# Attention groups put between the gate projections, in the second block of a two-block model

## What is computed

```
h = rms_norm_2(x, attn_norm_g[i])
proj = h @ w_in[i]
q, k, v, f_logit, cb, cc, cu, ga, gb = jnp.split(proj, offs, axis=-1)

q = rms_norm_2(q.reshape(b, s, N_ATT_HEADS, HEAD_DIM), q_norm_g[i])
k = rms_norm_2(k.reshape(b, s, N_ATT_HEADS, HEAD_DIM), k_norm_g[i])
log_f = jax.nn.log_sigmoid(f_logit.astype(jnp.float32) + b_f[i].astype(jnp.float32))
y_att = forgetting_attention(q, k, v, log_f)      # 8 heads of 64, causal, blocks of 128 queries

y_conv = cb * causal_short_conv(cc * cu, conv_w[i])

merged = (jax.nn.sigmoid(ga) * (y_att @ w_out_att[i])
          + jax.nn.sigmoid(gb) * (y_conv @ w_out_conv[i]))
x = x + merged @ w_o[i]
```

## Time and profile before

| | us |
|---|---|
| median of 3 runs | 1838.84 |
| lowest, highest | 1838.61, 1843.57 |
| the profiled execution | 1839.28 |
| its span in the profile | 1837.6 |

### The profile page before, as it was taken

One profiled execution on the slowest core, in us unless ns is written; L12 is line 12 of the kernel. 1 busy time (PEld: TensorE's weight loads), 2 busy tenths in 40 slices (PEclk: granted clock), 3 DMA queues, 4 the chain that ended last, 5 costly groups with the idle time before them and its releaser, 6 DMA issues.

```text
span 1837.6 us, 24106 instructions
## 1 busy us (share of the span) xinstructions
PE 1696.0 (92%) x9603; PEld 1372.4 (75%) x9603; DVE 1286.6 (70%) x1152; ACT 1000.6 (54%) x850; POOL 23.9 (1%) x37
## 2 busy tenths in 40 slices
PE   6989999997999999999999999999699978799977
PEld 6969998886676767767676766767499947688856
DVE  5974445895887878788787878878547424577773
ACT  4644433553776767667676767667334322266642
POOL 3000000000000000000000000000000000000000
PEclk9999999997999999999999999999899957799998
DMA  9535555422889979898997989898645502288850
GB/s 288 183 118 175 185 194 187 141 90 103 296 303 335 370 261 367 312 330 306 333 350 285 373 300 336 304 334 328 195 146 176 184 1 92 81 272 276 275 185 23
DMA packets 240762, 431.54 MB, mean 235 GB/s; under 512 B 11540, under 2 KB 121648, under 8 KB 240688
## 3 DMA queue, kind: packets, MB, share of 16 engines
q1 hardware_dynamic: 239200, 426.17, 66.0%
q10 hardware_dynamic: 1488, 4.34, 0.7%
HBM read 429.44 MB, written 1.05 MB: 234 GB/s over the span
## 4 chain that ended last, share of the span: by engine, by line
PE 74%; issue 14%; DVE 7%; ACT 3%; DMA 1%; POOL 0%; DVEq 0%; SPq 0%; POOLq 0%; ACTq 0%
PE PS L991 22%; PE PS L993 21%; PE PS L992 21%; DVE w_low L1433 2%; PE PS L1071 2%; PE PS L1205 2%; ACT w_high L799 2%; PE PS L1191 1%; DVE hT_low L1433 1%; PE PS L1370 1%; PE PS L1369 1%; PE PS L1237 1%; PE PS L1385 1%; DMA ring<-in_w_in_dram 1%; DVE yT_low L1433 1%
## 5 line engine op out<-in xcount | busy, mean ns | idle before, releaser
L1433 DVE TENSOR_TENSOR w_low<-ring,w_high 128x2048 fp32r<-128x2048 f32 x402 | 917.2, 2289 | 323.8 <-ACT w_high L663 169.4
L799 ACT ACTIVATE w_high<-ring 128x2048 fp32r<-128x2048 f32 x306 | 585.5, 1917 | 281.4 <-PE PS L993 281.2
L991 PE MATMUL PS<-w_high,hT_high 128*96 128x512 f32 (+3 forms) x1184 | 421.6, 356 | 13.1 <-DVE w_low L1433 8.0
L993 PE MATMUL PS<-w_high,hT_low 128*96 128x512 f32 (+3 forms) x1184 | 413.8, 349 | 0.0
L992 PE MATMUL PS<-w_low,hT_high 128*96 128x512 f32 (+3 forms) x1184 | 412.3, 348 | 0.0
L663 ACT ACTIVATE w_high<-ring 128x2048 fp32r<-128x2048 f32 x96 | 182.9, 1911 | 153.3 <-PE PS L993 149.5
L991 PE MATMUL PS<-w_high,yT_high 128*96 128x512 f32 (+1 forms) x568 | 228.9, 403 | 23.0 <-DVE yT_low L1433 23.0
L991 PE MATMUL PS<-hT_high,w_high 128*128 128x256 f32 x832 | 239.4, 288 | 8.2 <-DVE hT_low L1433 6.4
L991 PEld LDWEIGHTS PS<-w_high,hT_high 128*96 128x96 f32 (+1 forms) x1184 | 196.9, 166 | 64.9 <-DVE w_low L1433 7.7
L992 PE MATMUL PS<-hT_low,w_high 128*128 128x256 f32 x832 | 237.1, 285 | 0.0
L993 PE MATMUL PS<-hT_high,w_low 128*128 128x256 f32 x832 | 237.1, 285 | 0.0
(11 more groups left out here) (287 smaller groups left out, 1328.2 us busy)
## 6 DMA issues: line engine op xcount, KB each, us to landing
ring<-in_moe_wg_dram SPq DMA_DIRECT2D x88, 1024.0 KB, 6.1
ring<-in_moe_wu_dram SPq DMA_DIRECT2D x88, 1024.0 KB, 6.9
ring<-in_moe_wd_dram SPq DMA_DIRECT2D x80, 1024.0 KB, 5.7
ring<-in_w_in_dram SPq DMA_DIRECT2D x36, 1024.0 KB, 5.7
ring<-in_w_gate_dram SPq DMA_DIRECT2D x16, 1024.0 KB, 6.8
ring<-in_w_up_dram SPq DMA_DIRECT2D x16, 1024.0 KB, 7.7
ring<-in_w_down_dram SPq DMA_DIRECT2D x16, 1024.0 KB, 5.2
ring<-in_ffn_wg_dram SPq DMA_DIRECT2D x11, 1024.0 KB, 5.2
```

The lines of the kernel that those rows point to most:

```text
L799: act.activation(w_high[:, (s.base + k) % SPLITS, :], slot(w), ACT.Copy).then_inc(s.high_taken, 1)
L991: mm(o, left_high, right_high, start=first, stop=False, skip_group_check=shared)
L993: return mm(o, left_low, right_high, start=False, stop=last_one, skip_group_check=shared)
L1433: return tt(out_, whole, part.bitcast(F32), ALU.subtract)
```

## The change

TensorE now computes the first logits behind the `cu` tiles, and the rest of the attention in between the eight gate tiles: logits 0, gate 0, logits 1, gates 1 and 2, transposed weights 0, gate 3, weighted values 0, gate 4, transposed y 0 and weights 1, gate 5, weighted values 1, gate 6, transposed y 1, gate 7. The gates use banks 4 and 5 in turn, with one sigmoid of 512 columns per tile; block 0 of the attention uses banks 6 and 7, block 1 banks 0 to 3. ScalarE's and VectorE's lists are put in the matching order, with one `high` or `low` between two steps. `w_out_conv2` and `w_out_att` stand behind each other after the last gate. A new semaphore, `out_att_half`, tells when the first four of eight column chunks of `w_out_att` are complete; VectorE merges the first half on it and the second after the last chunk. `w_o` sums into banks 4 to 7 (before 0 to 3), its first two tiles wait for the first half of the merge alone, and there are 8 idle transposes in place of 16. What each operation computes stays as it was.

```diff
+            def gate(k):
+
+                name = (("ga0", "ga1", "gb0", "gb1")[k // 2], k % 2)
+                used(act, name)
+                act.activation(sgu[:, k // 2, (k % 2) * HALF:(k % 2 + 1) * HALF], bank(4 + k % 2),
+                               ACT.Sigmoid).then_inc(gates_act, 1)
+
...
+            gate(0)
+            high(B + 15)
+            weights_of(0)
+            gate(1)
+            high(B + 16)
+            act.wait_ge(yconv, 1)
+            act.activation(yT_high[:, 4:8, :].rearrange("p c s -> p (c s)"), wk[2], ACT.Copy).then_inc(yconv_high, 1)
+            gate(2)
+            high(B + 17)
+            turned_weights(0)
+            gate(3)
+            high(B + 18)
+            weights_of(1)
+            gate(4)
+            high(B + 19)
+            y_high(0)
+            turned_weights(1)
+            gate(5)
+            high(B + 20)
+            gate(6)
+            high(B + 21)
+            y_high(1)
+            gate(7)
+            high(B + 22)
+            high(B + 23)
...
-            for name, b, freed, value in (("cc", 0, qk_hat, 1), ("cu", 2, qk_hat, 2), ("ga0", 4, cbu_copied, 1),
-                                          ("ga1", 6, qk_std, 2), ("gb0", 0, cc_used, 1), ("gb1", 2, cbu_copied, 2)):
-                pe.wait_ge(freed, value)
+            for name, b, value in (("cc", 0, 1), ("cu", 2, 2)):
+                pe.wait_ge(qk_hat, value)
                 for hf in range(2):
                     project_T((name, hf), b + hf)
+
+            def logits(t):
+
+                n, each, b0 = P * (t + 1), 4 // (t + 1), 0 if t else 6
+                for hd in range(HEADS):
+                    o = PS[:, b0 + hd // each, (hd % each) * n:(hd % each + 1) * n]
+                    mm(o, qz[:, hd, t * P:(t + 1) * P], uT[:, hd // 2, 0:n], start=True, stop=False)
+                    last = mm(o, head_row[0:HEADS, hd, :], negc[:, 0:n], start=False, stop=True)
+                last.then_inc(att_logits, 1)
...
+            def turn_weights(t):
+
+                L, nk = (L1 if t else L0), t + 1
+                pe.wait_ge(att_exp, HEADS * (t + 1))
...
+            def weighted_values(t):
+
+                nk = t + 1
+                pe.wait_ge(att_pT_s, (1, 3)[t])
+                pe.wait_ge(att_pT_v, (1, 3)[t])
...
+            def turn_y(t):
+
+                pe.wait_ge(att_y, t + 1)
+                for c in range(4):
+                    last = nc.tensor.transpose(PS[:, 1 if t else 7, c * P:(c + 1) * P],
+                                               wk[3][:, t * HALF + c * P:t * HALF + (c + 1) * P], ident[:])
...
+            def gate(k):
+
+                if k >= 2:
+                    pe.wait_ge(gates_act, k - 1)
+                project_T((("ga0", "ga1", "gb0", "gb1")[k // 2], k % 2), 4 + k % 2)
+
+            pe.wait_ge(qk_std, 2)
+            logits(0)
+            pe.wait_ge(cbu_copied, 1)
+            gate(0)
+            pe.wait_ge(cbu_copied, 2)
+            pe.wait_ge(cc_used, 1)
+            logits(1)
+            gate(1)
+            gate(2)
+            turn_weights(0)
+            gate(3)
+            weighted_values(0)
+            gate(4)
+            turn_y(0)
+            turn_weights(1)
+            gate(5)
+            weighted_values(1)
+            gate(6)
+            turn_y(1)
+            gate(7)
...
+                        if name == "out_att" and m == 1 and c == 3:
+                            last.then_inc(att_half, 1)
                     last.then_inc(split_used, 1)
 
             pe.wait_ge(yconv_low, 1)
-            pe.wait_ge(gates_act, 2)
+            pe.wait_ge(gates_act, 8)
+            pe.wait_ge(att_yT, 1)
             out_chunks("out_conv2", 4, 4)
...
             pe.wait_ge(att_yT, 2)
             out_chunks("out_att", 0, 0)
             pe.wait_ge(mT_sum, 1)
-            spare(4, 16)
-            pe.wait_ge(merged, 2)
+            pe.wait_ge(conv_gated, 2)
+            spare(4, 8)
             for m in range(4):
-                rows_of_model(("o", m), h_rows, 0, m == 0, m == 3)
+                pe.wait_ge(merged, 1 + m // 2)
+                rows_of_model(("o", m), h_rows, 4, m == 0, m == 3)
...
 
             v.wait_ge(cbu_copied, 2)
             cu = wk[1].rearrange("p (c s) -> p c s", c=CH)
             tt(cpad[:, :, PAD:], chunks(0), cu, ALU.mult).then_inc(cc_used, 1)
             v.wait_ge(cc_used, 1)
-            low(B + 15)
+            low(B + 14)
...
+            def row_maxima(t):
+
+                L, n, each, b0 = (L1 if t else L0), P * (t + 1), 4 // (t + 1), 0 if t else 6
+                v.wait_ge(att_logits, t + 1)
...
+            row_maxima(0)
...
+            low(B + 15)
+            row_maxima(1)
             low(B + 16)
-            low(B + 17)
-            low(B + 18)
             v.wait_ge(yconv_high, 1)
             rest_of(yT_low[:, 4:8, :].rearrange("p c s -> p (c s)"), wk[2],
                     yT_high[:, 4:8, :].rearrange("p c s -> p (c s)")).then_inc(yconv_low, 1)
-            for T in range(19, 24):
-                low(B + T)
+            low(B + 17)
+            turned_weights(0)
+            low(B + 18)
+            scaled_y(0)
+            low(B + 19)
+            y_low(0)
+            turned_weights(1)
+            low(B + 20)
+            scaled_y(1)
+            low(B + 21)
+            y_low(1)
+            low(B + 22)
+            low(B + 23)
...
-                        yT_high[:, 0:4, t * P:(t + 1) * P]).then_inc(att_yT, 1)
-
             low(B + 24)
             low(B + 25)
-            used(v, ("out_att", 1))
-            v.wait_ge(conv_gated, 2)
-            for k in range(2):
+
+            def merge(k):
+
                 own.link(tt(sgu[:, k, :], sgu[:, k, :], bank(2 * k, 2), ALU.mult))
                 tt(sgu[:, k, :], sgu[:, k, :], sgu[:, 2 + k, :], ALU.add).then_inc(mT_sum, 1)
-            for k in range(2):
+
+            def merged_low(k):
+
                 v.wait_ge(mT_high, k + 1)
                 rest_of(hT_low[:, 4 * k:4 * k + 4, :].rearrange("p c s -> p (c s)"), sgu[:, k, :],
                         hT_high[:, 4 * k:4 * k + 4, :].rearrange("p c s -> p (c s)")).then_inc(merged, 1)
+
+            v.wait_ge(conv_gated, 2)
+            v.wait_ge(att_half, 1)
+            merge(0)
+            used(v, ("out_att", 1))
+            merge(1)
+            merged_low(0)
+            merged_low(1)
             for T in range(26, 30):
                 low(B + T)
-            add_rows(0, 3, ("o", 3))
+            add_rows(4, 3, ("o", 3))
...
```

More of the change, by code:

```diff
@@ L276, in build @@
         rows_half, conv_gated, yconv_low = sem("rows_half"), sem("conv_gated"), sem("yconv_low")
+        att_half = sem("out_att_half")
         rest_landed = [[sem(f"rest{k}_landed{s}") for s in range(SLOTS)] for k in (1, 2)]
@@ L908, in _, with weights_of @@
             high(B + 14)
[L909 to L919, removed]
+            def gate(k):
[3 more added lines that the diff above has]
+                               ACT.Sigmoid).then_inc(gates_act, 1)
+            def weights_of(t):
                 L = L1 if t else L0
@@ new lines, in turn_weights @@
+            def turn_weights(t):
+                L, nk = (L1 if t else L0), t + 1
+                pe.wait_ge(att_exp, HEADS * (t + 1))
+                for b in range(2 * nk):
+                    for c in range(4):
+                        hd, kt = (4 * b + c) // nk, (4 * b + c) % nk
+                        last = nc.tensor.transpose(PS[:, (0 if t else 6) + b, c * P:(c + 1) * P],
+                                                   L[:, hd, kt * P:(kt + 1) * P], ident[:])
+                    last.then_inc(att_turned, 1)
@@ new lines, in weighted_values @@
+            def weighted_values(t):
+                nk = t + 1
+                pe.wait_ge(att_pT_s, (1, 3)[t])
+                pe.wait_ge(att_pT_v, (1, 3)[t])
+                for hd in range(HEADS):
+                    for kt in range(nk):
+                        last = mm(PS[:, 0 if t else 6, hd * 64:(hd + 1) * 64], PT[:, hd * nk + kt, :],
+                                  vn[:, kt, hd * 64:(hd + 1) * 64], start=(kt == 0), stop=(kt == nk - 1))
+                last.then_inc(att_out, 1)
@@ new lines, in turn_y @@
+            def turn_y(t):
+                pe.wait_ge(att_y, t + 1)
+                for c in range(4):
+                    last = nc.tensor.transpose(PS[:, 1 if t else 7, c * P:(c + 1) * P],
+                                               wk[3][:, t * HALF + c * P:t * HALF + (c + 1) * P], ident[:])
+                last.then_inc(att_yturned, 1)
+            def gate(k):
+                if k >= 2:
+                    pe.wait_ge(gates_act, k - 1)
+                project_T((("ga0", "ga1", "gb0", "gb1")[k // 2], k % 2), 4 + k % 2)
@@ L1857, in _ @@
                 op1=ALU.mult).then_inc(qk_hat, 1)
-            for T in range(10, 15):
+            for T in range(10, 14):
                 low(B + T)
@@ L1890, in _ @@
             for k in range(2):
```

(10 more changed lines are left out.)

76 lines of the change are left out of this document (28 added, 48 removed).

## The result

| | before | changed |
|---|---|---|
| median, us | 1838.72 (4 runs) | 1814.76 (4 runs) |
| lowest, highest | 1838.37, 1843.57 | 1812.80, 1818.79 |
| the profiled execution | 1839.28 | 1815.69 |
| its span | 1837.6 | 1813.9 |
| mean granted clock | 0.959 | 0.966 |

The ratio is 0.9866, with a 95% interval of 0.9842 to 0.9890: 24.7 us faster by the ratio. The forecast was 1813, with 1801 to 1826 as its range.

The account below looks back on a forecast made before the run. TensorE's work was taken as the bound, leaving its idle and lower-clock time to win. 12.4 + 11.7 - 3.6 + 1.8 + 2.7 + 0.9 = 25.9 us off 1839.3 gave 1813 us, range 1801 to 1826.

Parts of the forecast that it names:

- Waits: TensorE's idle time in the attention: 13.2 us before, 1.5 us taken for the new order, so 11.7 less.
- Small groups at full clock: The attention's 32 transposes and 48 weighted-value records, at about 0.12 us each: 9.7 us in place of 18.6.
- Rival 2: The attention's small groups pull the clock down too, slowing them and later tiles: up to 1831 us; chance 0.09.
- First logits: The attention's first logits group: the clock falls 4.1 us in, as before, so it still takes 8.3 us.
- Second logits: The attention's second logits group: full clock at first, falling again after 4.1 us; 14.9 us in place of 18.4.
- rival 1: The clock holds: both logits groups run at full clock and no tile starts at half: 1803 us; chance 0.15.
- Gate tiles behind the logits: The gate tile behind each logits group starts at half clock, losing 1.8 us, twice: 3.6 us more.
- `w_out_att`, 1.8 less: Output product of the attention, now behind `w_out_conv2`: all at full clock, 1.8 us less.
- Merge: Pause from the end of `w_out_att` to the start of `w_o`: 4.6 us in place of 7.3, 2.7 less.
- The lower bound of 3.7: Shortest pause from `w_out_att` to `w_o` allowed for, with the merge's first half done in time: 3.7 us.
- `w_o`'s clock: Start of `w_o`, before 3.5 us at half clock losing 1.75: with a gap of 4.6, half saved, 0.9 less.
- The rule on idle gaps: Trainium skill's rule that idle gaps between bursts lower the clock; by it the clock would hold through both logits groups.

Follow-up runs that it names:

- 6: 3 with two tiny activations, each with a table switch, put ahead of ScalarE's second exponentials: 1801.27 us.
- number 1: The changed kernel with the old merge: both halves after all of `w_out_att`, `w_o` waiting for both, 16 idle transposes: 1816.45 us, ratio 0.9865.
- number 2: The kernel before with only `w_out_conv2` moved behind the attention, its gating and one high and low part with it: 1840.41 us, ratio 0.9994.
- Number 8: 3 with VectorE's list reordered: the merge's first half and its low part come ahead of the low part of tile 25: 1794.54 us, ratio 0.9750.
- number 7: 3 with the merge as it was before the change: 1800.92 us.
- 3: The changed kernel with the decay product of the logits at depth 128 instead of 8, added rows zero: 1797.96 us, ratio 0.9771.
- 4: The changed kernel with the logits cut into pieces of 2 to 4 heads, between halves of gate tiles: 1807.95 us, ratio 0.9820.
- 10: The changed kernel with the decay product at depth 64 instead of 8, added rows zero: 1805.23 us, ratio 0.9820.
- number 5: The kernel before with the decay product at depth 128, added rows zero: 1823.75 us, ratio 0.9915.
- number 9: The changed kernel measured once more, unaltered, with its own profile: 1815.63 us, ratio 0.9869.

## Why the prediction was right, point by point

- **Waits, 11.7 us less: right.** TensorE's idle time to the end of `w_out_att` is 1 us against the 1.5 I took, and the tight place was the one named (exponentials at 1467.49 for 1467.54; I had 0.4 us). Making them later costs its full length (6).
- **Small groups at full clock, 18.6 to 9.7: right,** at 0.12 us a record. Rival 2 did not occur in any profile.
- **First logits, 8.3: close.** 9.1 and 8.9 us in the two profiles of the changed kernel; the clock fell 3.1 and 3.5 us in, not 4.1.
- **Second logits, 14.9: one of two outcomes.** I took the fall as certain. One profile has 9.9 with the clock full to the last record (it fell as gate 1 began), the other 15.0, and number 1 also fell. This is rival 1 by half, in some executions. With it, one profile of the stretch gives 106.6 us and the other 112.9 (1412.55 to 1525.44); I had 111.7.
- **Gate tiles behind the logits, +3.6: right** in the first profile, 7.7 and 7.5 us for two tiles of 5.75, so +3.7. In the second, gate 0 took 8.1 us, and in gate 1 the clock came back only 5.7 us in.
- **`w_out_att`, 1.8 less:** the half clock there is gone (1.00 in its windows), but by number 2 this is a share of the interleaving, not of the product's move.
- **Merge, 7.3 to 4.6: right,** 4.55 us from 1515.2 to 1519.77, for the reason given: the low part of tile 25 ends at 1513.79, and only then comes the first half. The lower bound of 3.7 was too high: it kept the second half's sums ahead of the first half's low part. Number 8 takes both out of the way and gets 2.1. Undoing the halves costs 3.0 in number 7.
- **`w_o`'s clock, 0.9 less: wrong.** The step that failed is "With a gap of 4.6 I count half of it as saved": this pause gave no sure saving. In all six profiles with it (the changed kernel's two, 3, 4, 6 and 10) the clock fell in the pause or within 1.4 us behind it, and `w_o` ran 3.2 to 5.7 us at half clock, before 3.6. From the start of `w_o` to the next root the changed kernel took 27.5 us in one profile and 26.4 in the other, before 26.5, so 1.0 more or 0.1 less. At a pause of 2.1 (number 8) the clock held, and the same part took 24.9. I priced the half clock by the length of the pause, and these profiles don't bear that out.
- **The rule on idle gaps.** In numbers 3 and 10 the logits hold full clock and in the changed kernel they don't; in all three TensorE has no gap there, and only the depth of the decay product differs. It is so throughout: in the five profiles with depth 8 and whole groups (before, the changed kernel's two, 1 and 2) the clock fell inside the first logits, in the six with depth 64 or 128 in neither group. By the Trainium skill (TensorE: Matmul & The Clock Gate, HAM oscillation) idle gaps between bursts draw the clock down; the trace does not agree for this fall. It does agree in number 5, where the clock fell in the pause behind the logits.

The sum was 25.9 us; the medians give 24.0 (first measurement) and 24.6 (number 9). That the single number came within 2 us is in part luck. Of the sum, 25.0 lay in the stretch up to `w_o`. The first profile gained 30.1 there, since the second logits held the clock, and lost 6.4 elsewhere; the second gained 23.8. The range of the forecast held, since it was drawn to reach both outcomes of the clock; that the outcome would change from one execution to the next it did not say.

## What to carry to other kernels

Where three engines work in turns through small steps, spread the steps between independent dense tiles: the waits go, and so does the half clock behind them, here the whole gain of some 24.5 us less the 3 of the merge, at the price of in-order queues with hardly any margin. Look at shallow products that alternate with full ones: filled up with zero rows they took no longer and gained 17.5 us here (13.0 and 16.7 by the profiles' blocks), without touching the order of TensorE's work. And when a step is split in halves, put the first half's work, to its last part, ahead of everything in the queue that waits for something later; splitting the merge was worth 3.0 us with the first half behind a low part, and 3.4 more with it ahead.

## What I had not expected of the hardware

- **A product of fewer rows slows its full-depth neighbours.** Full clock, f32, alternating with a product of 128 rows: depth 128 takes 0.43 us for a pair of 256 columns, depth 64 and depth 8 both 0.63. The weight loads tell where it goes. Here are those of the full-depth product and its matmuls, first at depth 128 (number 3), then at 64 (number 10):

```profile
1422.12 0.41 PEld L1380 LDWEIGHTS PS<-uT,h 128*128 128x128 f32 x2
1422.34 0.59 PE L1380 MATMUL PS<-uT,h 128*128 128x256 f32 x2
```

```profile
1424.89 0.30 PEld L1380 LDWEIGHTS PS<-uT,h 128*128 128x128 f32 x2 [0.33 <-issue]
1424.89 0.70 PE L1380 MATMUL PS<-uT,h 128*128 128x256 f32 x2
```

  At depth 128 the loads start 0.22 us ahead of their matmuls, during the other product; at depth 64, and at 8, they start with them, after 0.33 us without a load. A single load takes as long in both cases (190 and 188 ns on average). So what is lost is the load ahead of time where the row counts change; why the engine doesn't do it there, stays open.
- **The clock can fall without any gap on TensorE.** It fell 3.1 to 4.2 us into the first logits at depth 8, not at depth 64 or 128, and only once when the pieces were cut finer (4). At depth 64 the records are as slow as at depth 8 and the clock holds, so it is not the slow records that bring it down. What in the shallow product does is not shown.
- **The fall is not the same in each execution of one program.** The second logits kept the clock in one profile and lost it in another. The changed kernel's nine runs lie within 12 us. What decides between the two outcomes stays open.
- **The same block of unchanged code ahead of the change** ended anywhere between 1315.8 and 1322.0 us. The unchanged code behind norm 6 took 262.5 to 268.8 us. A difference of a few us between two profiles needs reference points that leave such code out.
